# A float32 two-block model on one core: where the squares of a norm are summed, who rounds the operands, how many PSUM banks lead a stage, and q, k, v computed token by token

## What is computed

```python
h = rms_norm(x, norm1_g)
proj = jnp.einsum('bsd,de->bse', h, w_in)
q, k, v, bg, cg, xc = jnp.split(proj, ...)        # 1024 columns each
q = rms_norm(q.reshape(b, nc, CHUNK, N_HEADS, HEAD_DIM), q_norm_g)
k = rms_norm(k.reshape(b, nc, CHUNK, N_HEADS, HEAD_DIM), k_norm_g)
```

## Time and profile before

| | us |
|---|---|
| median of 3 runs | 2638.17 (2632.98 to 2641.39) |
| the profiled execution, own time | 2636.76 |
| its span, first to last instruction | 2635.0 |
| TensorE busy | 2485.9 (94%) |
| TensorE weight loads (beside it) | 2019.5 (77%) |
| VectorE busy | 1651.5 (63%) |
| GpSimd busy | 1370.3 (52%) |
| ScalarE busy | 481.8 (18%) |

### The profile page before, as it was taken

The page is one execution under the profiler, slowest core; times in us unless marked ns, Lnnn a source line. Parts: engine busy times, 40 slices in busy tenths (PEclk is TensorE's granted clock), DMA queues, the critical chain, the costliest instruction groups (busy, mean ns, idle before and its releaser), DMA issues.

```text
span 2635.0 us, 32100 instructions
## 1 busy us (share of the span) xinstructions
PE 2485.9 (94%) x12340; PEld 2019.5 (77%) x12340; DVE 1651.5 (63%) x2144; ACT 481.8 (18%) x1015; POOL 1370.3 (52%) x773
## 2 busy tenths in 40 slices
PE   7989999999999999888989999989899988999997
PEld 5767778887788876677768888868778876788885
DVE  7847764325904326577469994165788883899913
ACT  2103321000000000245210000023445431100000
POOL 6544446665656664344346666634243434466661
PEclk9989999999999999989999999989899999999998
DMA  4222222223222222112122222312111211232231
GB/s 148 80 72 89 85 76 96 96 97 104 88 96 96 96 89 72 64 57 65 59 70 96 96 96 96 97 55 73 40 65 57 65 48 64 67 100 98 96 96 56
DMA packets 59755, 214.58 MB, mean 81 GB/s; under 512 B 6624, under 2 KB 6752, under 8 KB 59488
## 3 DMA queue, kind: packets, MB, share of 16 engines
q1 hardware_dynamic: 56880, 206.68, 23.7%
q10 hardware_dynamic: 2736, 5.96, 0.7%
HBM read 210.51 MB, written 2.10 MB: 81 GB/s over the span
## 4 chain that ended last, share of the span: by engine, by line
PE 78%; DVE 18%; ACT 2%; issue 2%; DMA 0%; DVEq 0%; SPq 0%; ACTq 0%
PE acc L491 22%; PE acc L493 22%; PE acc L492 22%; PE ps_s L613 2%; DVE rstd L1215 2%; PE ps_o L635 2%; PE ps_t L570 2%; PE ps_t L623 2%; DVE u_hi L1203 1%; PE ps_s L836 1%; DVE hg_level_k L1697 1%; DVE hg_in L1649 1%; DVE hg_level_q L1697 1%; DVE u_tmp L1476 1%; DVE u_lo L1205 1%
## 5 line engine op out<-in xcount | busy, mean ns | idle before, releaser
L449 POOL CAST w_hi<-w_raw 128x1024 fp32r<-128x1024 f32 x384 | 413.3, 1076 | 1186.5 <-DMA w_raw<-stream 1186.5
L452 POOL TENSOR_TENSOR w_lo<-w_raw,w_hi 128x1024 fp32r<-128x1024 f32 x384 | 957.1, 2493 | 30.7
L491 PE MATMUL acc<-h_hi,w_hi 128*128 128x512 f32 (+1 forms) x2144 | 868.3, 405 | 29.8 <-DVE h_lo L1209 24.6
L493 PE MATMUL acc<-h_hi,w_lo 128*128 128x512 f32 (+1 forms) x2144 | 829.2, 387 | 0.0
L492 PE MATMUL acc<-h_lo,w_hi 128*128 128x512 f32 (+1 forms) x2144 | 827.5, 386 | 0.0
L491 PEld LDWEIGHTS acc<-h_hi,w_hi 128*128 128x128 f32 x2144 | 407.9, 190 | 126.9 <-DVE h_lo L1209 31.4
L492 PEld LDWEIGHTS acc<-h_lo,w_hi 128*128 128x128 f32 x2144 | 407.9, 190 | 88.2 <-issue 13.4
L493 PEld LDWEIGHTS acc<-h_hi,w_lo 128*128 128x128 f32 x2144 | 406.3, 189 | 82.7
L1246 DVE COPY y_all<-acc 128x512 f32<-128x512 f32 x32 | 22.1, 692 | 213.4 <-PE acc L493 212.0
L947 ACT ACTIVATE square<-x_res 128x512 f32<-128x512 f32 x48 | 30.3, 633 | 609.7 <-DVE x_res L1482 273.8
L493 PE MATMUL acc<-hid_hi,w_lo 128*128 128x512 f32 x352 | 137.0, 389 | 0.0
(11 more groups left out here) (252 smaller groups left out, 3456.0 us busy)
## 6 DMA issues: line engine op xcount, KB each, us to landing
w_raw<-stream SPq DMA_DIRECT2D x384, 512.0 KB, 3.3
toeplitz<-ext_in ACTq DMA_DIRECT2D x16, 256.0 KB, 3.7
out<-x_res SPq DMA_DIRECT2D x4, 512.0 KB, 2.7
x_res<-x_in SPq DMA_DIRECT2D x3, 512.0 KB, 6.8
mem<-mem_in ACTq DMA_DIRECT2D x1, 1024.0 KB, 4.8
consts<-consts_in SPq DMA_DIRECT2D x1, 784.0 KB, 9.8
x_res<-x_in SPq DMA_DIRECT2D x2, 256.0 KB, 5.1
rope<-rope_in ACTq DMA_DIRECT2D x1, 512.0 KB, 5.7
```

The lines of the kernel that those rows point to most:

```text
L449: nc.gpsimd.tensor_copy(hi, raw).then_inc(hi_made, 1)
L452: nc.gpsimd.tensor_tensor(lo, raw, f32(hi), ALU.subtract).then_inc(split_made, 1)
L491: nc.tensor.matmul(ps, hi, x_hi[:, k, 0:cols], start=(k == 0), stop=False)
L493: mm = nc.tensor.matmul(ps, lo, x_hi[:, k, 0:cols], start=False, stop=(k == st.kt - 1))
```

## The change

1. **Norm squares.** For the inputs of `up0`, `a_in`, `ffn_in0` and `ffn_in1`, ScalarE squares each tile (`x_square`), VectorE adds the eight squares into `rstd_in` (`x_sum`), and TensorE makes a single ones-product of the sum (`summed_norm`): after k = 3 of the lead in `up0` and `a_in`, after the fifth block in `ffn_in`. The inputs of `qkv`, `b_in` and the memory keep their eight products.
2. **Rounding on ScalarE.** ScalarE makes `h_hi` (`x_half`), `u_hi` and its square, and `hid_hi`; VectorE keeps only the subtractions (`x_rest`, `u_rest`, `hidden_rest`). They run interleaved with the blocks of the stage before: tiles of x for `a_in` are made as `down1` ends each of them. Tile 0 for `up0` has buffers of its own (`x0_hi`, `x0_lo`), since `h_hi` is still read by stage `out`. In `add_norm` the product for tile i+1 is put ahead of the rest of tile i.
3. **Seven leading banks.** In `ffn_in0` and `ffn_in1` (`WIDE`) blocks 4, 5 and 6 go to `ps_s0`, `ps_s1` and `ps_o`, so seven blocks need no eviction. The token products use the same seven banks.
4. **Token-major q, k, v.** Stage `qkv` becomes six stages of four blocks. The stationary operand is now `h` of 128 tokens, the moving one 512 columns of weights; the result has tokens on partitions. ScalarE squares a bank, VectorE sums by head (`tensor_reduce`, 128x8), ScalarE takes the root, VectorE inverts 128x8 and multiplies the bank; TensorE turns it back with four transposes per bank (q and k only), ScalarE copies with the gain. v is copied by ScalarE straight to `v_tok1`. The 1/rms of the tokens is turned to a column by four transposes of `rms`. The first two score pairs are issued inside the last group.
5. **Recurrence.** ScalarE's exponentials of the second direction move behind the copy of `hg_v`.

The core of the diff:

```diff
+def place_accumulators(stages, names):
+            extra = name in WIDE and BANKS <= c < BANKS + EXTRA
+            bank = c if extra else turn % BANKS
...
+            def summed_norm():
+                n["rms"] += 1
+                n["x"] += 1
+                take_t(rms_ready, n["rms"])
+                pe.wait_ge(x_sq_used, DT * n["x"])
+                nc.tensor.matmul(ps_t[:], const("ones"), rstd_in[:], start=True, stop=True).then_inc(x_summed, 1)
...
+            def tokens(g, x_hi, x_lo, ready, then):
+                st = stages[TOKENS[g]]
+                for s in range(st.slots):
+                    slot = st.first_slot + s
+                    pe.wait_ge(split_made, slot + 1)
+                    for b in range(BLOCKS):
+                        i, cols = g * BLOCKS + b, slice(b * P, (b + 1) * P)
+                        if s == 0 and token_free(i) is not None:
+                            pe.wait_ge(*token_free(i))
+                        for half in range(2):
+                            k = 2 * s + half
+                            if ready is not None and b == 0:
+                                ready(k)
...
+                            nc.tensor.matmul(out_, x_hi[:, k, cols], hi, start=(k == 0), stop=False)
+                            nc.tensor.matmul(out_, x_lo[:, k, cols], hi, start=False, stop=False)
+                            mm = nc.tensor.matmul(out_, x_hi[:, k, cols], lo, start=False, stop=(k == st.kt - 1))
...
+                        then(s * BLOCKS + b)
+            def first_sums(at):
+                for i in {3: [0, 1], 7: [2, 3, 4], 11: [5, 6, 7]}.get(at, []):
...
+                    sum_square(i, DT, const("ones"))
+                if at == 13:
...
+                        mm = nc.tensor.transpose(ps_t[:, b * P:(b + 1) * P], rms[:, b * P:(b + 1) * P], const("ident"))
...
+            def first_scores(at):
+                if at in (3, 7):
+                    pe.wait_ge(qk_ready, 4 * BLOCKS)
+                    pe.wait_ge(stages["v0"].free, BLOCKS)
+                    scores(units1, at // 4)
...
             def conv_mlp(layer):
+                st = stages[f"ffn_in{layer}"]
+                lead(st, h_hi, h_lo, waits_for(h_ready, n["h"]))
+                for c in range(BANKS, st.cbs):
+                    block_at(st, c, h_hi, h_lo)
+                    if c == BANKS:
+                        summed_norm()
...
+            for i in range(2 * HALF):
+                t_ = u_tmp[:, i % 2, :]
+                act.wait_ge(stages[f"up{i // HALF}"].free, i % HALF + 1)
+                nc.scalar.activation(t_, t_, ACT.Square).then_inc(u_squared, 1)
...
+                act.wait_ge(u_squared, i + 1)
+                nc.scalar.activation(u_hi[:, i % HALF, :], t_, ACT.Copy).then_inc(u_hi_made, 1)
...
+                head_rest(h, 0)
                 if h:
                     head_square(h - 1)
                 act.wait_ge(vt_done, v0 + h + 1)
                 nc.scalar.activation(hg_v[:].rearrange("p b n -> p (b n)"), ps_t[:], ACT.Copy).then_inc(v_ready, 1)
+                head_rest(h, 1)
...
+                scaled_y(0)
                 for i in range(DT):
                     step.wait()
+                    step(nc.vector.tensor_tensor(x_res[:, i, :], x_res[:, i, :], normed[:, i % 2, :], ALU.add), x_ready)
+                    if i < DT - 1:
+                        scaled_y(i + 1)
+                    rest(i)
+                    if next_gain is not None and summed:
+                        x_sum(i)
```

More of the change, by code:

```diff
@@ L53 @@
 BLOCK_CHUNKS = P // HG_CHUNK
-LEAD = {"qkv", "up0", "memkv", "a_in", "a_out", "ffn_in0", "b_in", "b_out", "ffn_in1"}
+TOKENS = ["q0", "q1", "k0", "k1", "v0", "v1"]
+WIDE = {"ffn_in0", "ffn_in1"}
+EXTRA = 3
+LEAD = {*TOKENS, "up0", "memkv", "a_in", "a_out", "ffn_in0", "b_in", "b_out", "ffn_in1"}
 STAGES = [
-    ("qkv", 24, 8), ("conv", 24, 8), ("gate", 16, 8), ("proj", 16, 8), ("out", 8, 8),
+    *[(name, BANKS, 8) for name in TOKENS], ("conv", 24, 8), ("gate", 16, 8), ("proj", 16, 8), ("out", 8, 8),
     ("up0", HALF, 8), ("down0", 8, HALF), ("up1", HALF, 8), ("down1", 8, HALF),
@@ L113, in made @@
         return self.first_slot + ((c + 1) * self.kt - 1) // SLOT_TILES + 1
-    def bank(self, c):
-        return (self.first_cb + c) % BANKS
+def place_accumulators(stages, names):
+    last, turn = {}, 0
+    for name in names:
+        st = stages[name]
+        st.banks, st.before = [], []
+        for c in range(st.cbs):
+            extra = name in WIDE and BANKS <= c < BANKS + EXTRA
+            bank = c if extra else turn % BANKS
+            turn += not extra
+            st.banks.append(bank)
+            st.before.append(None if extra else last.get(bank))
+            if not extra:
+                last[bank] = (st, c)
 class Order:
@@ L304, in build @@
             s.free = sem(f"free_{s.name}")
+        place_accumulators(stages, [name for name, _, _ in STAGES if name not in TOKENS])
+        banks = [*acc, *ps_s, ps_o]
         dve_own = sem("dve_own")
@@ new lines, in turn_tokens @@
+            def turn_tokens(g, at):
+                if at in (2, 4, 6, 8):
+                    b = at // 2 - 1
+                    i = g * BLOCKS + b
+                    take_t(qk_ready, i + 1)
+                    pe.wait_ge(stages[TOKENS[g]].free, b + 1)
+                    for c in range(BANKS):
+                        cols = slice(c * P, (c + 1) * P)
+                        mm = nc.tensor.transpose(ps_t[:, cols], qk_tok[:, i % 2, cols], const("ident"))
+                    mm.then_inc(qk_turned, 1)
@@ L688, in _ @@
             for half in range(2):
-                looped(stages[f"up{half}"], 4, h_hi, h_lo, ready=waits_for(h_ready, n["h"]),
-                       then=input_norm if half == 0 else None)
+                looped(stages[f"up{half}"], 4, up_hi, up_lo, ready=waits_for(h_ready, n["h"]), then=early_norm)
                 looped(stages[f"down{half}"], 4, u_hi, u_lo, ready=waits_for(u_ready, half * HALF))
@@ L1082, in gelus, with next_input @@
                     nc.scalar.activation(t_, t_, ACT.Gelu_apprx_tanh).then_inc(gelu_ready, 1)
-            norm(x_res, stages["down1"].free, 0)
+                    act.wait_ge(hid_made, layer * FF2 + i + 1)
+                    nc.scalar.activation(hid_hi[:, i, :], t_, ACT.Copy).then_inc(hid_hi_made, 1)
+            def next_input(gain, summed=True):
+                first = DT * n["next"]
+                n["next"] += 1
+                for i in range(DT):
+                    act.wait_ge(x_ready, first + i + 1)
+                    x_half(i, gain)
+                    if summed:
+                        x_square(i)
+                    else:
+                        squared(x_res[:, i, :])
+                if summed:
+                    x_root()
+                else:
+                    root(n["sq"], 1.0 / D, small["eps_d"][:])
+            for i in range(DT):
+                act.wait_ge(stages["down1"].free, i + 1)
+                x_half(i, lambda i: param("norm_g", i))
+                x_square(i)
+            x_root()
             def mem_squares(tiles):
@@ L1245, in take @@
                 step.wait()
-                step(nc.vector.tensor_copy(dst, acc[st.bank(c)][:]), st.free)
+                step(nc.vector.tensor_copy(dst, banks[st.banks[c]][:]), st.free)
             def take_y(st, sq):
```

368 lines of the change are left out of this document (252 added, 116 removed).

## The result

The changed kernel takes 2592.1 us, median of four runs (2590.1 to 2594.3), against 2636.0, also of four, for the kernel before, measured beside it: a ratio of 0.983, 95% interval 0.981 to 0.985. The gain is 44 us where 62.3 were forecast. The profiled execution took 2592.6 us with a span of 2590.8.

What follows compares the result with a forecast made beforehand. TensorE, busy 94% of the span, was taken to bound the kernel. The terms 30 + 10.6 + 6.8 + 9.4 + 3.8 - 0.3 + 2 = 62.3 us, taken from 2636.8, gave 2574.5 us; range 2559 to 2600.

Steps and rivals of the forecast that it cites:

- the low ends: The smallest gains of all terms, 20 + 8 + 5 + 8 - 2 - 0.3 + 0 = 38.7 us, so 2598.
- the waits at the token borders: In q, k, v: TensorE held by late banks, 4 us at each of five borders; the forecast took none.
- part 5: `ffn_in0`, `ffn_in1`: seven of eight ones-products go, but VectorE holds the lead; +1.9 us each, 3.8 together, between +2.1 and -1 each.
- part 6: The rest: `b_in` starts later, -0.3 us; the heads lose the `hg_v` wait, 2 us taken, bounds 0 and 14.9.
- Part 1: q, k, v: token form drops products and transposes and hides the tail before `conv`; gain 30 us, range 20 to 31.
- the first rival: q, k, v: the token chain closes behind the banks, holding TensorE at five borders; price 20 us, 2594; chance 0.15.
- the rival of the slower swapped operands: q, k, v: products with swapped operands cost more; at 0.42 us each the price is 115 us, 2690; chance 0.04.
- Part 2: `up0`: the lead starts at once on tile 0, with one ones-product; gain 10.6 us, 8 if GpSimd blocks VectorE again.
- Part 3: `down0`: TensorE's wait for the last `u_lo` and the low clock around it go; gain 6.8 us, 5 at least.
- Part 4: `a_in`: six tiles are ready during `down1` and the lead shortens to 22.6 us; gain 9.4 us, 8 at least.
- The rival of the flickering leads: `ffn_in0`, `ffn_in1`: TensorE waits per tile and the clock drops, 9.6 us each, maybe `up0` too; 2593; chance 0.07.

Runs made afterwards that it cites:

- the arena set right: The changed kernel with the arena (the on-chip memory holding the stages' buffers) begun 192 bytes later and nothing else: 2584.8 us, ratio 0.980.
- the order alone: The kernel before with only ScalarE's second set of exponentials of each head moved behind the square and the copy of `hg_v`: 2645.8 us, ratio 1.003.
- The experiment that mends the three misses: The changed kernel with the arena 192 bytes later, ScalarE's old order in the heads and six-block leads in `ffn_in0` and `ffn_in1`: 2571.3 us, ratio 0.974.
- the six-block lead: The changed kernel with the lead of `ffn_in0` and `ffn_in1` six blocks wide in place of four: 2582.3 us, ratio 0.979.

## Why the prediction was right or wrong

The time, 2592.1, lies in the range of 2559 to 2600, and the sign was right; the forecast of 2574.5 was 17.6 us too fast. The measured time lies near the slow end of the range, for reasons that were not what the low ends were made of: of those, the waits at the token borders, 10 us, did not come, and of the losses that did come all but the one in part 5 were outside of their term's bounds (part 6) or in no term. That the range held is in part luck. By its own terms, in the profiled executions:

- **Part 1, 30 us: 29.0.** The stage itself fell by 26.5, the start by 0.5, `conv` by 2.0 for the clock. TensorE waits for no token bank at any border, so the first rival fell. The products of the token stages step by 0.227 us (the median), so the rival of the slower swapped operands fell too. The wait for ScalarE in the first group was 1.1 and 1.7 in two places, 1.7 forecast for one.
- **Part 2, 10.6: 9.7** with `out`, and 10.5 with the arena set right.
- **Part 3, 6.8: 6.0**, and 6.8 with the arena set right.
- **Part 4, 9.4: 9.5** with down1.
- **Part 5, +3.8: -0.1.** The bounds were +2.1 to -1 per stage and held; the value taken was wrong. It came from the mean of the sum's row, 1.18, and the paragraph had set the blocked slot beside it. The row after shows 0.69 in four places and 2.69 in three, and that lumps cost more than their mean: behind them TensorE waits 4.4 us and gets the lower clock. By the rule of the Trainium skill, "SBUF — State Buffer", section "Who interferes with whom", on VectorE instructions with two SBUF inputs beside GpSimd there was no gain to be had here, and the trace agrees with it: L1444 took 2.69 us in place of 0.69 in three places, each beside a split of GpSimd. The prediction counted the old rounding among the instructions with two such inputs. Its row reads one tile and a column of `params`; but GpSimd held it up all the same (the row in the section on the leads), so two roundings of 2.50 us became three sums of 2.69. The rival of the flickering leads was right in kind. Its size was not: it gave 9.6 a stage, and the lower clock, 3.4 us long, costs about 1.6 (8 products at 0.2). With what the Trainium skill tells in "TensorE: Matmul & The Clock Gate", section "HAM oscillation — how this bites in real kernels", of waits between bursts that bring the low clock back, this trace agrees: the granted clock is 0.88 in this lead and 0.95 where the waits were filled.
- **Part 6, 1.7: -7.1.** This is the step that failed most. "TensorE's wait then only moves" was right, and VectorE's wait for ScalarE was read rightly as a sign that VectorE bounds the head. But the bound of the term was put at 0 from below, for no reason that excluded a loss. The forecast named VectorE's 1.95 us wait for ScalarE's logarithm and did not ask what the move does to it: three exponentials now stand behind ScalarE's wait for TensorE, and that wait grew from 7.1 to 13.5 us over six heads with the order alone. Nor was the end of the last head in the term, where 3.7 of the loss lie. The size of the whole by fourteen profiles is 5.5 us; the rest, 1.6, is within what the heads vary by with one order. Of the term itself, +1.7, nothing came.
- **Not in the sum: -4.5 in proj, up1, ffn_out0 and ffn_out1**, and 0.7 to 0.9 each in up0, down0 and down1. up1 lost more than proj (1.2 to 0.9), because a block's first tile at another distance slows nine products behind it too; why stays open. The price of a stream product was taken as a constant, 0.226 us, and the six tables in the diff were taken as free. By the experiment the whole item is 7 to 9 us, half of the 17.6.
- **Also not in the sum:** memkv and a_out, 1.7 shorter. Over the kernels memkv took 138.8 to 144.2 us with nothing changed in it, so nothing is read from this.

The sum is 29.0 + 9.7 + 6.0 + 9.5 - 0.1 - 7.1 - 4.5 + 1.7 = 44.2, and the spans give 2635.0 - 2590.8 = 44.2. The experiment that mends the three misses, 2571.3, is within 3 us of the forecast, by other means in part 5.

## What to carry to other kernels

Where three engines wait for one another in a ring, serving TensorE first can take the time from whoever is queued behind that favour; follow the ring once around, and let the term go below nothing. Where one engine makes tiles for TensorE in lumps, widen the step in between rather than thin out TensorE's own work: the six-block lead gave 4.8 to 5.0 us a stage where the removed ones-products gave none. And read the allocations of a diff as part of it: after a change compare the step of products in a stage that it does not touch.

## What the runs showed of the hardware

- The step of a 128x512 product depends on where its moving operand lies against the weights: 226.7 ns at a distance of a multiple of 256 bytes, 228.9 at 64 beyond one, 233.3 at 128 beyond, at the full granted clock and with no wait (proj in the kernels above). Moving weights and operands together changed nothing. In proj it repeats to 0.01 us over 87 us. In up1 of the kernel after, nine products at a distance of 0 behind three at 64 stepped by 231 ns as well.
- A wait of TensorE of 2.68 us (L940 in the kernel after), and two of 2.27 and 2.14 with twelve products between them (its `ffn_in0`), were followed by the lower clock; in rows 9 a single one of 2.67 was not.
- VectorE's sum of two SBUF operands took 0.69 or 2.7 us and nothing in between in the lead of `ffn_in0` of the kernel after; beside each of the three long ones GpSimd was splitting weights (L503, 2.71 us from 1305.57 beside the first).
